# Merge gates in sixteen pieces inside two attentions, with levels, norms and old states reordered, in a decoder trunk

## The chip, the cores and the metric

The kernel runs on one core of a Trainium2 chip. TensorE (PE), VectorE (DVE), ScalarE (ACT), GpSimd (POOL) and SyncE (SP) each follow their own instruction list and meet at semaphores; SP's list here is a queue of DMA issues. The metric is the device time of one execution in microseconds. For the kernel before it is 1652.79 us, the median of 3 runs (1651.17 to 1656.56).

## The reference

One layer of a hybrid decoder for 256 prompt tokens and 8 x 4 sample tokens (288 rows of 1024, float32). The rows are multiplied by `W_in` (1024 x 5400), whose columns are the NSA queries, keys, values and branch gates, the HGRN2 parts `hq`, `hf`, `hi`, `hg`, and two merge gates of 1024 columns each. Then

```
a = NSA(z)     # compressed blocks + 16 selected blocks + window of 512, gated
b = HGRN2(z)   # gated linear recurrence, 4 heads of 128 x 128 states
h = LN1(alpha*x + (sig(g_a) * (a @ W_pa) + sig(g_b) * (b @ W_pb)) @ W_o)
y = LN2(alpha*h + MoE(h))   # router, top 4 of 32 experts, clamped SwiGLU
```

The sample tokens also read a paged cache (1024 past positions for each of 8 sequences) and an old HGRN2 state. The new states and cache rows are outputs too.

## The kernel before

The whole kernel is one hand-ordered list per engine; there is no planner. The order is what the code of each engine's block says, and waits on semaphores tie the lists together. The stages in TensorE's order:

- **Projection.** Eleven column blocks (`BLOCKS`) of 512 columns are loaded through three slots of `big`. A group (`GROUPS`) is one 128-column piece (turned: output columns on partitions, 288 tokens free; L633) or one token tile (L647; the 32 sample rows in four column groups, L641). Groups go through `NB` = 5 PSUM banks and are copied out by ACT or DVE. The last four blocks, `ga` and `gb`, are the merge gates: 16 groups, copied into `gates` by ACT (L1113).
- **HGRN2 levels.** The intra-chunk part is summed over seven levels (`LEVELS`). Level n needs, in turn: a difference on DVE (`half_diff`), Abs and Exp on ACT (L1146, L1148), one product on DVE (`hqF`, L1520) and one on GpSimd (`hkF`, L1344), the scores on TensorE (`level_scores`, L608), and mask and sum on DVE (`add_level`). `LEVEL_AFTER` puts the scores after every second merge gate group.
- **Compression.** Eight sequences in three sets (`CMP_SETS`). For each set pages are transposed (L675) and copied by both ACT (L1171) and DVE (L433), two hidden products for each of k and v (L688), Gelu on ACT, and small products for block keys and values.
- **HGRN2 states and outputs** (L728 to L768).
- **Prompt attention** in four steps `ITS` (query tile, head pair): `prompt_scores` (L810, and L813 for block scores), `prompt_max` on DVE, `prompt_exp` on ACT (eight row groups at L1207, four of 15 block columns at L1210), `prompt_weigh` on DVE, `prompt_turn` (L829, L832) with copies by ACT (L1219), `prompt_values`. In steps 2 and 3 `sample_gain` (L793) adds new keys to the old states, which GpSimd has decayed (L1358) and DVE adds up (`add_gain`, L1655); then the states are stored.
- **Sample attention** in two halves `s` of 16 tokens: small scores, twelve transposed key blocks (L886) and their scores, a selection on DVE after an importance product (L893), softmax over ACT and DVE, transposed probabilities (L904), values (L925), one last transpose (L928). SP loads the rows with `load_rows(0)` and `load_rows(1)` (L508: pages, L510: windows); the second waits for `pv_done` and for the stored old states.
- **Merge and output.** Eight column pieces (L940), gated by DVE (L1803), then `w_o` (L947) for three token tiles in two halves, residual (L1836), `norm` over all three tiles phase by phase (L1813 to L1828), transposes (L962), router product (L968), selection.
- **Experts.** 32 experts in a loop, each with four pairs of gate/up buffers (2 MB each) and four of down buffers (1 MB each). A buffer is loaded again when TensorE frees it (`gu_free`, `dn_free`, waited for by SP in `load_gu`, `load_dn`). Before the loop both semaphores are raised once `w_o` is through. L1027 is gate/up, L1057 down, `combine` (L1013) brings an expert's rows back and DVE adds them (`add_rows`, L1911).
- **Tail.** Three last combines, each waiting for the additions before it, `norm` on `y_rows`, three stores by GpSimd's queue.

## Time and profile before

| | |
|---|---|
| median of 3 runs | 1652.79 us (1651.17 to 1656.56) |
| profiled execution | 1650.89 us, span 1649.1 us |
| TensorE busy | 1455.6 us, 88% of the span |
| DVE, ACT, GpSimd busy | 431.8, 300.9, 80.5 us |
| moved from HBM | 471.54 MB |

The profile is one execution. Times are from the start of the span. A matmul of float32 is two records of TensorE, so that 32 records are 16 products. "Clock" is what the throttle granted of 2.4 GHz as a mean over the stretch (1.00 is 2.4 GHz, 0.50 would be 1.2 GHz). A row of busy time by stretch gives the stretch, its length, then the busy us (and instructions) of PE, PEld (weight load), DVE, ACT and POOL, the clock, the mean busy share of the DMA engines and GB/s. A row of groups by form gives line, engine and operation, out and in, and behind the bar its busy us and the mean ns of one, then idle time before it and what ended that. A releaser behind `<-` is the instruction whose semaphore ended a wait.

### The profile page before, as it was taken

The numbers are of one execution on the slowest core, as the hardware profiler recorded it, in microseconds if no ns is written. First come the engines' busy times: TensorE is split into PE (matmuls) and PEld (weight loads), VectorE is DVE, ScalarE is ACT, GpSimd is POOL, SyncE is SP. The second block draws the span as 40 slices with busy tenths as digits, with TensorE's granted clock in tenths as the row PEclk, the third lists the DMA queues.
The fourth block names the chain that finished last, engine by engine and source line by source line (L and its number), as shares of the span: only waits on it lengthen the run. The fifth ranks groups of instructions, "written<-read, shape, count | busy, mean of one in ns | idle before, by whom it ended". The sixth has DMA issues, their size and how long they took to land.

```text
span 1649.1 us, 20185 instructions
## 1 busy us (share of the span) xinstructions
PE 1455.6 (88%) x7423; PEld 654.3 (40%) x7423; DVE 431.8 (26%) x861; ACT 300.9 (18%) x545; POOL 80.5 (5%) x107
## 2 busy tenths in 40 slices
PE   6999988995755977999999999999999999999993
PEld 4757745574433624333333333323323323323321
DVE  0314432027422223221222212212212222222225
ACT  0103332014322012111111111111111111111111
POOL 0102300002000000000000000000000000000000
PEclk9999989997677996999999999999999999999997
DMA  6962120105155425999999999999999999999970
GB/s 235 335 212 103 32 77 23 29 22 175 33 165 151 160 92 233 420 417 417 418 416 418 419 414 418 418 417 418 417 415 418 412 405 419 409 405 419 410 313 30
DMA packets 116827, 476.52 MB, mean 289 GB/s; under 512 B 10451, under 2 KB 32275, under 8 KB 83827
## 3 DMA queue, kind: packets, MB, share of 16 engines
q1 hardware_dynamic: 112976, 465.78, 71.8%
q0 software_dynamic: 1856, 8.59, 1.5%
q10 hardware_dynamic: 1954, 1.63, 0.3%
q8 instruction: 24, 0.39, 0.1%
q14 instruction: 17, 0.13, 0.0%
HBM read 471.54 MB, written 8.59 MB: 291 GB/s over the span
## 4 chain that ended last, share of the span: by engine, by line
PE 49%; DMA 35%; DVE 8%; issue 2%; ACT 2%; SPq 2%; POOL 1%; DVEq 0%; ACTq 0%; POOLq 0%
DMA big<-in_w_gu 34%; PE bank L1027 14%; PE bank L688 7%; PE bank L633 5%; PE bank L1057 5%; PE bank L647 3%; PE bank L947 3%; PE bank L940 2%; PE bank L1013 2%; DVE big L433 1%; DVE work L1911 1%; PE bank L630 1%; DMA big<-in_w_in 1%; SPq L507 1%; SPq L508 1%
## 5 line engine op out<-in xcount | busy, mean ns | idle before, releaser
L1027 PE MATMUL bank<-big,gates 128*64 128x512 f32 x2048 | 451.1, 595 | 24.5 <-DMA big<-in_w_gu 23.7
L1027 PEld LDWEIGHTS bank<-big,gates 128*64 128x64 f32 x2048 | 142.1, 137 | 310.8 <-issue 257.1
L1057 PE MATMUL bank<-big,gates 128*64 128x512 f32 x1024 | 226.8, 595 | 0.0
L1911 DVE TENSOR_TENSOR work<-work,bank 128x512 f32<-128x512 f32 x198 | 127.0, 683 | 279.3 <-PE bank L1013 279.3
L1893 DVE TENSOR_SCALAR gates<-bank 128x512 f32<-128x512 f32 x32 | 22.1, 692 | 455.4 <-PE bank L1039 455.4
L1013 PE MATMUL bank<-gates 64*128 64x512 f32 x396 | 111.8, 641 | 21.0 <-DVE work L1911 21.0
L1057 PEld LDWEIGHTS bank<-big,gates 128*64 128x64 f32 x1024 | 70.7, 137 | 133.3 <-issue 133.3
L688 PE MATMUL bank<-big 128*128 128x417 f32 (+2 forms) x384 | 116.8, 464 | 4.6 <-DVE big L433 4.6
L1301 ACT ACTIVATE gates<-gates 128x512 f32<-128x512 f32 x32 | 20.2, 630 | 474.3 <-DVE gates L1893 474.3
L633 PE MATMUL bank<-xT,big 128*128 128x288 f32 x384 | 95.3, 407 | 0.0
L688 PEld LDWEIGHTS bank<-big 128*128 128x128 f32 x384 | 72.8, 191 | 46.5 <-issue 21.4
L1367 POOL TENSOR_TENSOR gates<-gates,nsaT 128x192 f32<-128x192 f32 x64 | 31.4, 511 | 1102.1 <-PE bank L1066 912.7
L633 PEld LDWEIGHTS bank<-xT,big 128*128 128x128 f32 x384 | 72.2, 190 | 20.0 <-issue 0.6
L994 PE MATMUL bank<-work,gates 128*64 128x512 f32 x264 | 65.5, 618 | 0.0
L1309 ACT ACTIVATE gates<-bank 128x512 f32<-128x512 f32 x32 | 19.1, 597 | 239.6 <-PE bank L1013 239.6
L1013 PEld LDWEIGHTS bank<-gates 64*128 64x128 f32 x396 | 29.8, 184 | 82.5 <-issue 51.9
L647 PE MATMUL bank<-big,xT 128*128 128x512 f32 (+1 forms) x128 | 51.5, 562 | 2.0 <-DMA big<-in_w_in 2.0
L947 PE MATMUL bank<-big,qT 128*128 128x512 f32 (+1 forms) x96 | 41.6, 593 | 1.5 <-DVE qT L1805 1.5
L1301 ACT ACT_TABLE_LOAD x32 | 41.1, 1283 | 0.6
L987 PE MATMUL bank<-work,gates 32*64 32x512 f32 x132 | 36.3, 627 | 3.0 <-DVE gates L1885 3.0
L647 PEld LDWEIGHTS bank<-big,xT 128*128 128x128 f32 x128 | 24.6, 194 | 26.5 <-issue 25.1
L1039 PE MATMUL bank<-kv,const 1*64 1x512 f32 x256 | 34.8, 613 | 0.0
(336 smaller groups left out, 1163.4 us busy)
## 6 DMA issues: line engine op xcount, KB each, us to landing
big<-in_w_gu SPq DMA_DIRECT2D x128, 2048.0 KB, 23.1
big<-in_w_dn SPq DMA_DIRECT2D x128, 1024.0 KB, 21.2
big<-in_w_in SPq DMA_DIRECT2D x10, 2048.0 KB, 14.7
big<-in_cache_cmp_kv SPq DMA_DIRECT2D x64, 128.0 KB, 2.5
big<-in_cache_slc_kv SPq DMA_DIRECT2D x64, 128.0 KB, 2.1
big<-in_cache_win_kv SPq DMA_DIRECT2D x8, 512.0 KB, 3.6
big<-in_w_o SPq DMA_DIRECT2D x1, 4096.0 KB, 12.9
out_win_s<-in_cache_win_kv POOLq DMA_DIRECT2D x1, 4064.0 KB, 6.9
```

The costliest lines, as they stand in the source:

```text
L633: last = pe.matmul(bank[:, 0:NT], w[:, k, n * P:(n + 1) * P], xTv[:, k, :], start=(k == 0), stop=(k == KD - 1))
L647: last = pe.matmul(bank[0:m, 0:cols], xTv[:, k, t0:t0 + m], w[:, k, 0:cols], start=(k == 0), stop=(k == KD - 1))
L688: last = pe.matmul(psum[3 + m][:, 0:n], w1[:, v, l, m * P:(m + 1) * P], XT[:, v, l % 8, l // 8:l // 8 + n], start=(l == 0), stop=(l == LP ...
L947: last = pe.matmul(psum[(4 + i) % 8][0:m, :], mixT[:, k, t0:t0 + m], w_o[:, k, (i % 2) * 512:(i % 2 + 1) * 512], start=(k == 0), stop=(k = ...
L987: pe.matmul(psum[0][half * CAP:(half + 1) * CAP, :], pick_rows[0:NS, 2, :], h_rows[0:NS, 2, half * 512:(half + 1) * 512], start=True, stop ...
L994: last = pe.matmul(psum[0][half * CAP:(half + 1) * CAP, :], pick_rows[:, t, :], h_rows[:, t, half * 512:(half + 1) * 512], start=False, st ...
L1013: last = pe.matmul(psum[6 + half][:, :], pgT[rows, t, :], ye[rows, :], start=True, stop=True)
L1027: last = pe.matmul(psum[2 + n][half * CAP:(half + 1) * CAP, :], xe[:, k % 4, (k // 4) * CAP:(k // 4 + 1) * CAP], gu_slot[k][:, c0:c0 + 512 ...
L1039: last = pe.matmul(psum[2 + n][half * CAP:(half + 1) * CAP, :], C("ones")[row, 0:CAP], bias[row, half * 512:(half + 1) * 512], start=False ...
L1057: last = pe.matmul(psum[5][half * CAP:(half + 1) * CAP, :], act_T[:, k % 4, (k // 4) * CAP:(k // 4 + 1) * CAP], dn_slot[k][:, half * 512:( ...
L1301: act.activation(sg, g_lim, ACT.Sigmoid, scale=1.702).then_inc(sg_ready, 1)
L1911: dve.tensor_tensor(y, y, psum[6 + half][:, :], ALU.add).then_inc(y_added, 1)
```

## The change

- The merge gates leave `BLOCKS`. They become 16 groups `gate_group(f)` of their own, f from 0 to 15, with weights in eight loads of 1 MB (`load_gates`, slots `wg_slot`). Gates 0 to 7 stand in the prompt attention and use bank 4 with DVE copying; gates 8 to 15 stand in the two halves of the sample attention, use bank 6, and ACT copies. Each waits for the copy of the one before (`fill_copied`). The sigmoid over all gates follows the last one.
- Level scores 0 to 2 stand between the `hi` and `hg` groups, 3 to 6 in the first compression set, between its pages and hidden products. Block keys and values use bank 7 and move one place later. The sets run over the sequences in another order (`CMP_ORDER`).
- The old states' `sample_gain` and `add_gain` stand ahead of `prompt_scores(0)`. Block scores of all four steps are made at once (`block_scores`, `block_shift`, one exponential, `block_weigh`) instead of within each step.
- SP loads selected rows per sequence (`load_rows(s, b4)`) and windows apart (`load_window`); the second half's rows overlay the old states and are split into those that wait for `state_p_stored` and those that wait for `states_stored`.
- `dn_free` is raised after the sample attention, half of `gu_free` after the merge, the other half after `w_o`.
- The sample rows of `w_o` run in four column groups at the start. The norms use `bn_stats` and `bn_aggr` tile by tile, in the order sample, prompt tile 0, prompt tile 1, beside `w_o`, transposes and router products. In the tail the last combines have banks of their own, norms run by tile, and SP stores.
- Several tiles move in SBUF to make room.

```diff
-CMP_SETS = [(0, 3), (3, 3), (6, 2)]
+CMP_SETS = [(5, 3), (2, 3), (0, 2)]
+CMP_ORDER = [b0 + n for b0, nb in CMP_SETS for n in range(nb)]
...
+LN_ORDER = [2, 0, 1]
+LAST_BANKS = [6, 2, 0]
...
           ("hf", C_HF, 512, True), ("hq", C_HQ, 512, True), ("hi", C_HI, 512, False),
-          ("hg", C_HG, 512, False), ("ga", C_GA, 512, True), ("ga", C_GA + 512, 512, True),
-          ("gb", C_GB, 512, True), ("gb", C_GB + 512, 512, True)]
+          ("hg", C_HG, 512, False)]
...
-LEVEL_AFTER = [n for n, g in enumerate(GROUPS) if g[0] in ("ga", "gb")][1::2][:len(LEVELS)]
+LEVEL_AFTER = [GROUPS.index(("hi", 5, 0)), GROUPS.index(("hg", 6, 0)), GROUPS.index(("hg", 6, 2))]
+NF = 2 * KD
...
+        wg_slot = [part(big, at, [KD, 2 * P]) for at in (8192, 10240, 8192, 10240, 20480, 22528, 8192, 10240)]
...
+            def load_gates(n):
+
+                sp.dma_start(wg_slot[n], ins["w_in"][0, :, C_GA + 2 * P * n:C_GA + 2 * P * (n + 1)].rearrange("(k p) n -> p k n", p=P))\
+                  .then_inc(w_loaded[1 + n % 2], 16)
+
+            sp.wait_ge(page_used, 6)
+            load_gates(0)
+            load_gates(1)
...
             sp.wait_ge(c_done, 6)
-            load_rows(0)
+            load_rows(0, 0)
+            load_rows(0, 1)
+            sp.wait_ge(fill_done, 2)
+            load_gates(2)
+            load_rows(0, 2)
+            sp.wait_ge(fill_done, 4)
+            load_gates(3)
+            load_rows(0, 3)
+            for b4 in range(4):
+                if b4 % 2 == 0:
+                    sp.wait_ge(fill_done, 6 + b4)
+                load_window(0, b4)
             sp.wait_ge(pv_done, len(ITS))
+            load_gates(4)
+            load_gates(5)
+            sp.wait_ge(state_p_stored, 16)
+            load_rows(1, 2)
+            load_rows(1, 3)
             sp.wait_ge(states_stored, 16 * DB)
-            load_rows(1)
-
+            load_rows(1, 0)
+            load_rows(1, 1)
+            sp.wait_ge(fill_done, 12)
+            for b4 in range(4):
+                load_window(1, b4)
+
+            sp.wait_ge(spv_done, 1)
+            load_gates(6)
+            load_gates(7)
...
             for k in range(KD // 2):
                 load_dn(0, 0, k)
-            for k in range(KD // 2):
+            sp.wait_ge(c_done, 6)
+            sp.dma_start(w_router[:, :, :], ins["w_router"][0].rearrange("(k p) n -> p k n", p=P)).then_inc(router_loaded, 16)
+            sp.dma_start(b_router, ins["b_router"].partition_broadcast(P).rearrange("p a n -> p (a n)")).then_inc(router_loaded, 16)
+            for k in range(KD // 4):
                 load_gu(0, 0, k)
...
+            sp.wait_ge(h_ready, 6)
...
+            for u in range(3):
+                turn_pages(u)
+                if u == 0:
+                    level_scores(3)
+                else:
+                    block_keys(2 * u - 1)
+                hidden(2 * u, 0)
+                if u == 0:
+                    level_scores(4)
+                hidden(2 * u, 1)
+                if u == 0:
+                    level_scores(5)
+                hidden(2 * u + 1, 0)
+                if u == 0:
+                    level_scores(6)
+                block_keys(2 * u)
+                hidden(2 * u + 1, 1)
 
...
-                    pe.wait_ge(ps_step, 5 * len(ITS))
-                    pe.wait_ge(ps_act, PREV_ACT[-1])
+                    pe.wait_ge(khat_ready, 3)
+                    pe.wait_ge(state_step, HH * (SEQ // CH))
...
+            def block_scores():
+
+                pe.wait_ge(state_step, HH * (SEQ // CH))
+                for it, (qt, hp) in enumerate(ITS):
+                    for hh in range(2):
+                        last = pe.matmul(psum[4][:, 4 * NCP * it:4 * NCP * (it + 1)].rearrange("p (g h c) -> p h g c", g=G, h=2)[:, hh, :, :],
+                                         qT[:, 0, 2 * hp + hh, qt * P:(qt + 1) * P], ckTp, start=True, stop=True)
+                last.then_inc(pcs_step, 1)
+
...
+            def gate_group(f):
+
+                pe.wait_ge(w_loaded[1 + f // 2 % 2], 16 * (f // 4 + 3))
+                pe.wait_ge(fill_copied, f + 1)
+                bank = psum[4 if f < 8 else 6]
+                for k in range(KD):
+                    last = pe.matmul(bank[:, 0:NT], wg_slot[f // 2][:, k, f % 2 * P:(f % 2 + 1) * P], xTv[:, k, :],
+                                     start=(k == 0), stop=(k == KD - 1))
+                last.then_inc(fill_done, 1)
...
+            block_scores()
+            sample_gain(0)
+            gate_group(0)
+            sample_gain(1)
             prompt_scores(0)
+            gate_group(1)
             prompt_scores(1)
             turn_outputs()
+            gate_group(2)
             for it in range(len(ITS)):
                 prompt_turn(it)
                 if it + 2 < len(ITS):
                     prompt_scores(it + 2)
-                else:
-                    sample_gain(it - 2)
                 prompt_values(it)
+                gate_group(3 + it)
+            gate_group(7)
...
+                pe.wait_ge(cc_step, 4 * s + 3)
+
+                pe.matmul(psum[0][:, 256:256 + NCS], C("same_group"), s_rows[:, 1600:1600 + NCS], start=True, stop=True).then_inc(cc_step, 1)
+                gate_group(8 + 4 * s)
+                gate_group(9 + 4 * s)
...
+                gate_group(10 + 4 * s)
+                gate_group(11 + 4 * s)
...
+            pe.wait_ge(spv_done, 4)
+            pe.sem_inc(dn_free, KD)
...
+            pe.wait_ge(ab_done, KD)
+            pe.sem_inc(gu_free, KD // 2)
...
-            for i in range(6):
-                t0, m = TILES[i // 2]
+            for k in range(KD):
+                for c in range(4):
+                    last = pe.matmul(psum[4][NS * c:NS * (c + 1), 0:D // 4], mixT[:, k, SEQ:NT], w_o[:, k, c * D // 4:(c + 1) * D // 4],
+                                     start=(k == 0), stop=(k == KD - 1), skip_group_check=True)
+            last.then_inc(wo_done, 1)
...
+            LOGIT_BANK = (1, 4, 5)
+            out_product(0)
+            out_product(1)
+            turn_h(0)
+            out_product(2)
+            pe.wait_ge(router_loaded, 32)
+            router_product(0)
+            out_product(3)
+            pe.wait_ge(wo_done, 5)
+            pe.sem_inc(gu_free, KD // 2)
+            turn_h(1)
+            router_product(1)
+            turn_h(2)
+            router_product(2)
...
+                for n, (b3, v, l) in enumerate(units[u]):
+                    turns = UNITS_BEFORE[u] + n
+                    act.wait_ge(xt_turned, turns + 1)
+                    copy_turned(lambda o, i: act.activation(o, i, ACT.Copy), u, b3, v, l, 0, turns).then_inc(xt_act, 1)
+
+            def gelu(q, m):
+
+                n = SET_N[q // 2]
+                if q:
+                    act.wait_ge(c_done, q)
+                act.wait_ge(hid_done, 2 * q + m + 1)
+                if q < 2:
+                    act.wait_ge(codes_copied, 2 * q + m + 2)
+                act.activation(hidT[:, m, 0:n], psum[3 + m][:, 0:n], ACT.Gelu_apprx_tanh,
+                               bias=pe_bias[:, q % 2, m:m + 1]).then_inc(gelu_done, 1)
...
+                copy_units(u)
+                if u == 0:
+                    level_decay(4)
+                    level_decay(5)
+                gelu(2 * u, 0)
+                if u == 0:
+                    level_decay(6)
+                gelu(2 * u, 1)
+                if u == 0:
+                    act.wait_ge(qf_ready, 6)
+                    act.wait_ge(kf_ready, 6)
+                    act.activation(hF[:, :, :], hb[:, :, :], ACT.Exp).then_inc(eb_ready, 1)
+                gelu(2 * u + 1, 0)
+                if u == 0:
+                    act.wait_ge(kd_diff, 2)
+                    act.activation(hkF[:, :, :], hkF[:, :, :], ACT.Exp).then_inc(kd_ready, 1)
+                gelu(2 * u + 1, 1)
...
+            act.wait_ge(pcs_step, 2)
+            act.activation(pcs, pcs, ACT.Exp, scale=SCALE).then_inc(pcs_step, 1)
             prompt_exp(0)
...
+                act.wait_ge(fill_done, f + 1)
+                act.activation(gatesT[:, f, :], psum[6][:, 0:NT], ACT.Copy).then_inc(fill_copied, 1)
...
                                    accum_out=stat[:, 3, 6 + n:7 + n]).then_inc(exp_done, 1)
+                    if n == 0:
+                        take_gates(8 + 4 * s)
...
+            def block_shift():
+
+                step = own.chain("pc_step", 0)
+                dve.wait_ge(pcs_step, 1)
+                mask = C("cmp_mask").rearrange("p (q c) -> p q c", q=2).unsqueeze(2).broadcast_to([P, 2, 8, NCP])
+                dve.tensor_tensor(pcs, psum[4][:, 0:16 * NCP].rearrange("p (q n c) -> p q n c", q=2, n=8), mask, ALU.add).then_inc(fill_copied, 1)
+                dve.wait_ge(fill_copied, 1)
+                step(dve.tensor_reduce(pc_stat[:, 0, :, :], pcs, AXX, ALU.max))
+                dve.tensor_tensor(pcs, pcs, pc_stat[:, 0, :, :].unsqueeze(3).broadcast_to([P, 2, 8, NCP]), ALU.subtract).then_inc(pcs_step, 1)
+
+            def block_weigh():
+
...
+            def take_gates(f):
+
+                dve.wait_ge(fill_done, f + 1)
+                dve.tensor_copy(gatesT[:, f, :], psum[4][:, 0:NT]).then_inc(fill_copied, 1)
+
+            block_shift()
+            add_gain(0)
+            take_gates(0)
+            add_gain(1)
             prompt_max(0)
+            take_gates(1)
             prompt_max(1)
+            block_weigh()
             outputs()
             for it in range(len(ITS)):
                 prompt_weigh(it)
+                take_gates(2 + it)
                 if it + 2 < len(ITS):
                     prompt_max(it + 2)
-                else:
-                    add_gain(it - 2)
                 prompt_out(it)
+            take_gates(6)
+            take_gates(7)
...
+            def norm_stats(rows, t, half):
+
+                m = TILES[t][1]
+                dve.bn_stats(ln_parts[0:m, t, half, :], rows[0:m, t, half * 512:(half + 1) * 512]).then_inc(own.next("ln_step"), 1)
+
+            def norm_scale(t, at):
+
+                m = TILES[t][1]
+                dve.wait_ge(own.semaphore, own.count)
+                dve.bn_aggr(ln_mean[0:m, t, :], ln_parts[0:m, t, :, :]).then_inc(own.next("ln_step"), 1)
+                dve.wait_ge(own.semaphore, own.count)
+                dve.tensor_scalar(ln_rstd[0:m, at % 3:at % 3 + 1], ln_mean[0:m, t, 1:2], LN_EPS, None, ALU.add).then_inc(ln_var, 1)
+
+            def norm_apply(rows, t, at, g, b, ready):
+
+                m = TILES[t][1]
+                rstd = ln_rstd[0:m, at % 3:at % 3 + 1]
+                dve.wait_ge(ln_rms, at + 1)
+                dve.reciprocal(rstd, rstd).then_inc(own.next("ln_step"), 1)
+                for half in range(2):
+                    cols = slice(half * 512, (half + 1) * 512)
+                    x = rows[0:m, t, cols]
+                    dve.scalar_tensor_tensor(out=x, in0=x, scalar=ln_mean[0:m, t, 0:1], in1=g[0:m, cols],
+                                             op0=ALU.subtract, op1=ALU.mult).then_inc(own.next("ln_step"), 1)
+                    dve.wait_ge(own.semaphore, own.count)
+                    dve.scalar_tensor_tensor(out=x, in0=x, scalar=rstd, in1=b[0:m, cols], op0=ALU.mult, op1=ALU.add).then_inc(ready, 1)
+
...
+            for at, t in enumerate(LN_ORDER):
+                for half in range(2):
+                    if at:
+                        i = 2 * (at - 1) + half
+                        x = h_rows[:, t, half * 512:(half + 1) * 512]
+                        dve.wait_ge(wo_done, i + 2)
+                        dve.scalar_tensor_tensor(out=x, in0=x, scalar=ALPHA, in1=psum[(5 + i) % 8][:, :], op0=ALU.mult, op1=ALU.add).then_inc(own.next("res_step"), 1)
+                        dve.wait_ge(own.semaphore, own.count)
+                    norm_stats(h_rows, t, half)
+                norm_scale(t, at)
+                norm_apply(h_rows, t, at, ln1[:, 0, :], ln1[:, 1, :], h_ready)
...
-            norm(y_rows, 1, ln2[0], ln2[1], y_ready)
+            for t in range(3):
+                dve.wait_ge(comb_done, rounds * (3 * NE) + t + 1)
+                if t == 0:
+                    dve.wait_ge(y_added, rounds * (6 * NE) + 6)
+                for half in range(2):
+                    y = y_rows[:, t, half * 512:(half + 1) * 512]
+                    dve.tensor_tensor(y, y, psum[LAST_BANKS[t] + half][:, :], ALU.add).then_inc(y_added, 1)
+                for half in range(2):
+                    dve.wait_ge(y_added, rounds * (6 * NE) + 7 + 2 * t + half)
+                    norm_stats(y_rows, t, half)
+                norm_scale(t, 3 + t)
+                if t:
+                    norm_apply(y_rows, t - 1, 2 + t, ln2[0], ln2[1], y_ready)
+            norm_apply(y_rows, 2, 5, ln2[0], ln2[1], y_ready)
```

## Rows read from the trace of the kernel before

**Rows 1.** The page: span, and the chain that ended last by engine.
```profile
span 1649.1 us, 20185 instructions
...
PE 49%; DMA 35%; DVE 8%; issue 2%; ACT 2%; SPq 2%; POOL 1%; DVEq 0%; ACTq 0%; POOLq 0%
```

**Rows 2.** Busy time of the engines by stretch, eight of the stages.
```profile
125.70:203.50 77.80, 76.35 (x396) 61.59 (x392) 37.65 (x49) 23.88 (x33) 24.88 (x9) 1.00 0.21 68
203.50:368.00 164.50, 145.51 (x622) 95.47 (x622) 31.53 (x59) 36.35 (x52) 0.00 (x0) 0.96 0.12 35
...
381.60:451.30 69.70, 41.64 (x238) 27.32 (x235) 39.05 (x116) 33.64 (x124) 9.51 (x7) 0.66 0.28 84
451.30:486.60 35.30, 22.04 (x210) 15.51 (x210) 9.25 (x33) 11.91 (x24) 4.13 (x6) 0.76 0.58 167
486.60:533.00 46.40, 21.35 (x211) 14.40 (x211) 8.43 (x29) 12.01 (x24) 0.00 (x0) 0.71 0.52 143
...
607.30:634.20 26.90, 12.93 (x72) 11.90 (x72) 15.69 (x27) 9.34 (x17) 0.00 (x0) 0.59 0.97 389
634.20:652.20 18.00, 10.15 (x34) 5.40 (x34) 6.76 (x28) 4.88 (x9) 0.97 (x2) 0.57 0.29 120
1619.00:1649.10 30.10, 3.39 (x12) 0.90 (x12) 18.08 (x27) 5.12 (x10) 1.65 (x3) 0.62 0.11 39
```

**Rows 3.** The chain of waits in the expert loop: start, length, piece.
```profile
652.22 13.95 PE bank L1027 x64
...
1541.83 26.69 DMA big<-in_w_gu
...
1572.50 26.52 DMA big<-in_w_gu
```

**Rows 4.** Timeline of TensorE and ScalarE, and groups by form (busy us, mean ns).
```profile
59.97 15.79 PE L633 MATMUL bank<-xT,big 128*128 128x288 f32 x64
...
L1344 POOL TENSOR_TENSOR work<-work 128x1152 f32<-128x1152 f32 x6 | 22.8, 3795 | 105.1 <-ACT work L1148 99.8 <-PE bank L608 5.3
...
204.78 4.04 ACT L1154 ACTIVATE gates<-gates 128x4608 f32<-128x4608 f32 x1
208.84 1.28 ACT L1158 ACT_TABLE_LOAD   x1
210.14 1.16 ACT L1158 ACTIVATE work<-work 128x1152 f32<-128x1152 f32 x1
...
249.63 22.70 PE L688 MATMUL bank<-big 128*128 128x417 f32 x64
```

**Rows 5.** Groups by form: decay, addition of gains, block scores.
```profile
L1358 POOL TENSOR_TENSOR big<-big,work 128x1024 f32<-128x1024 f32 x4 | 7.6, 1932 | 1.2 <-PE bank L768 1.2
...
L1655 DVE TENSOR_TENSOR big<-big,bank 128x512 f32<-128x512 f32 x8 | 5.0, 683 | 12.2 <-PE bank L793 12.2
...
L813 PE MATMUL bank<-xT,qT 128*128 128x30 f32 x16 | 3.4, 342 | 0.0
```

**Rows 6.** Waits of TensorE, 381 to 533 us: in total, times, longest.
```profile
PE bank L904 <- DVE work L1783: 17.8, 2, 8.9
PE bank L832 <- DVE small L1704: 17.0, 4, 5.7
PE bank L886 <- DMA big<-in_cache_win_kv: 12.9, 1, 12.9
```

**Rows 7.** Timeline of SP's queue: issue of eight selected pages.
```profile
488.65 8.03 SPq L508 DMA_DIRECT2D big<-in_cache_slc_kv  x8
```

**Rows 8.** Sample rows: w_o product by form, projection on the timeline.
```profile
L947 PE MATMUL bank<-big,qT 128*32 128x512 f32 x32 | 13.9, 593 | 0.0
...
108.01 1.95 PE L641 MATMUL bank<-big,xT 128*32 128x128 f32 x64
```

**Rows 9.** Router product in the chain, and a reduction by form.
```profile
626.14 7.97 PE bank L968 x48
...
L1813 DVE TENSOR_REDUCE small<-work 128x1 f32<-128x1024 f32 x4 | 4.8, 1212 | 0.0
```

585 lines of the change are left out of this document (287 added, 298 removed).

## The prediction

> **What bounds the kernel now.** I read the page first: TensorE is busy 88% of the span, and the chain that ended last is half TensorE and a third weight transfers [rows 1]. That average mixes two parts, so the next view is the busy time by stage [rows 2]. Up to 652.2 us the kernel is one chain through projections, compression, two attentions, merge, norm and router; after it come 32 experts. The chain of waits shows what sets the second part: from the middle of the loop on, experts follow each other 30.7 us apart, each waiting 26.5 us for its last gate/up transfer [rows 3]. The expert loop is therefore a transfer stream in the end. But the stream can only run on once expert 0 frees its first buffers, 3.8 us after it starts, and all eight buffer pairs are full by then in both versions. So the loop is a block of fixed length hung on expert 0's first matmul at 652.2, and a microsecond gained ahead of that is one gained in the end.
>
> In the front part the stages differ [rows 2]: 125.7 to 203.5 TensorE is full (76.4 of 77.8 us, clock 1.00, that is 2.4 GHz), with 16 merge gate groups and seven level scores. In the prompt attention (381.6 to 451.3) it works 41.6 of 69.7 us, in the sample attention (451.3 to 533.0) 43.4 of 81.7, at a mean clock of 0.66 to 0.76, which is partly the 1.2 GHz level. That is about 66 us of idle TensorE for 62 us of gates.
>
> **Part by part.** *Gates leave the projection.* Four groups take 15.8 us [rows 4], so one 3.9 and sixteen 62.4. The levels (77.8 - 62.4 = 15.4 us, 1.4 of it waiting) stay; three go between hi and hg groups, four between the first hidden products. Is there time for their chain there? One level costs a GpSimd product of 3.8 us, a difference of 1.4 (as long as the DVE product beside it), then Abs and Exp of 1.16 each with a table load of 1.28 [rows 4]: 8.8 us against 13.2 us for a hidden product (half of the 22.7 us of a pair) and a score. It fits, and the merge sigmoid (4.0 us and its table load) no longer stands ahead of the page copies. Reordering block keys into the shadow of page copies fills more. TensorE idled 19.0 us in 203.5 to 368.0, 20.4 with the 1.4 above. Following copies, levels and products through in the new order leaves me 12.0, so the stage gives 62.4 + 8.4 = **70.8 us**. Bounds: all of the 20.4 gone (74.8 with the 8 us that I do not expect), or each level late.
>
> The new order switches between Gelu and Exp, six table loads more. Rows have 1.28 us for each, with the activation starting 1.3 us after the one before [rows 4], and they lie beside products. The Trainium skill (ScalarE: Activation LUTs, What ACT_TABLE_LOAD costs) counts 2.66 us for each switch, drain included; no row here shows the 1.38 us of drain. By that figure the last switch alone would delay the next page copies by about 1.4 us, and the sum would be 72.0.
>
> *Old states in front of the prompt attention.* GpSimd's decay takes 7.6 us [rows 5] after the HGRN outputs. It was hidden; now sample_gain(1) waits for add_gain(0), which waits for it, and prompt_scores(0) waits for both: 7.8 and 0.8 to the end of add_gain(0), 1.4 for sample_gain(1) (as it takes where it stands now), 2.5 for add_gain(1) [rows 5]: 12.5 us, with block scores and gate 0 inside. Behind that stands a chain on DVE and TensorE. Gate 1 delays prompt_scores(1), and gate 2 the first transposes, by 3.9 each. Gates 3 to 5 lie in waits for the weighing of 3 to 6 us [rows 6]; 1.7 stay uncovered. Gates 6 and 7 have nothing beside them, since DVE copies gate 7 before it makes q_own: 8.6. Back come the two add_gains out of steps 2 and 3 (5.0), the block columns' exponentials (eight ACT instructions fewer per step, of which I let 1.0 count, four times) and their scores on TensorE, 3.4 [rows 5]. 12.5 + 3.9 + 3.9 + 1.7 + 8.6 - 5.0 - 4.0 - 3.4 = 18.2, so 69.7 becomes 87.9: **-18.2**. Bounds: if gates 1, 2, 6 and 7 run at 1.2 GHz, 15.6 more; above, rival (a).
>
> *Sample attention.* After the importance product TensorE waited 8.9 us, twice, for the probabilities [rows 6]. Two gates of 7.8 would fit, but both use bank 6, and ACT copies the first only between its two exponentials: the second starts 21.1 us into the half and ends at 25.1, where the transposes began at 23.0, so 2.1 late. Gates 10, 11 (and 14, 15) stand after the values, ahead of the last transpose, uncovered: 8.3 each half. One wait disappears: 12.9 us for the second half's rows [rows 6]. They were issued after the old states were stored, each eight pages taking 8.0 us of SP's queue and over 1 for what is between [rows 7]. Now the states are stored long before; but SP comes to these rows only past gate 7, for which the first half's last windows wait. Its 32 pages then take 37 us, and their first use is 47 us later. The windows, which wait for gate 11, have the 5 us of eight key transposes. The first half goes from 35.3 to 45.7, the second from 46.4 to 43.9, both together from 81.7 to 89.6: **-7.9**. Of the other new items in SP's queue, eight gate loads of 1 MB, the tightest two follow those windows: landed some 11 us into the second half, due at 14. Merges: the sigmoid (5.3 us) runs beside the first one and delays the first mix by 0.4, nothing behind it: 0.
>
> *w_o.* The 32 sample rows took 32 records, 13.9 us of 41.6 [rows 8]. In four column groups of 32 they are like the projection's 64 records over 128 columns in 1.95 us [rows 8]; at 256 columns 3.6. Added inside: transposes and router product of the sample tile, 2.1. 41.6 becomes 33.5: **+8.1**.
>
> *Norm and router.* 26.9 us at 607.3 [rows 2]. Now only tile 1 is left after the last product: residual 0.7, statistics 0.7, small steps and root 1.0, halves 1.4 and 1.4, so 5.2. TensorE's own chain is as long by then and goes on: tile 0's transposes 2.6, its copy and router product 3.5 (three took 8.0 [rows 9]), tile 1's transposes and copy 2.0, product 2.7: 10.8. **+16.1**. bn_stats is in no row: for 512 columns I take 0.7, half of a 1.2 us reduction over 1024 [rows 9] and a start; bounds 0.2 and 1.3.
>
> *Tail.* Three combines waited for each other's additions, then came whole-tile norms: 30.1 us from 1619.0 [rows 2]. Now additions 3 x 1.3, statistics 3 x 1.4, small steps 3 x 0.5, two passes over 3 x 1024 columns 3 x 3.0, and the first combine: 19 to 20 us, then 5.3 to store as before. 30.1 to 25.6: **+4.5** (bounds +8.5 and +1 by bn_stats).
>
> Sum: 70.8 - 18.2 - 7.9 + 8.1 + 16.1 + 4.5 = 73.4. The profiled execution took 1650.9 us (1.8 beyond its span), giving 1577.5; it lies 1.9 below the median of the runs, 1652.8, giving **1579**.
>
> **Rivals.** (a) *The clock gives more back.* TensorE is at 85% in the prompt stage then, and stretches like that show 0.90 to 1.00 [rows 2]. A third of some 25 us would come off the path: 8 us, 1571. The Trainium skill (TensorE: Matmul & The Clock Gate, HAM oscillation) says that idle waits between bursts bring the lower clock back; the trace agrees, with 0.66 in the stage with the most short waits. Against: most waits of the path are DVE's and ACT's. 0.13.
> (b) *SP's queue is late.* If the pages take the pace of a full queue, the 12.9 us wait returns before the second half: 1592. For: a slack of 10 us after a schedule of four steps. 0.07.
> (c) *The levels starve TensorE.* A GpSimd product and a table load late for each of three levels, 3 x 5.1 = 15: 1594. For: ACT and DVE do page copies and levels in one order, so that each waits for the other. 0.07.
> (d) *No gain past the loop*: if the transfer stream and not expert 0's start sets the end, only the tail's 4.5 is left, 1648. Against: the stream stands still from 635 to 656 (DMA share 0.29 in 634.2 to 652.2 [rows 2]). 0.02.
> (e) *Slower.* The gates run at 1.2 GHz (7.8 us each) and wholly uncovered, 124 us, in attentions that also pay 12.5 for the states, and SP's wait stays. Against 95.0 of gains ahead and behind and 4.5 in the tail: 124.8 + 12.5 - 99.5 = 38, 1691. It decides from an average of 5.4 us uncovered per gate; I count 2.4. 0.01.
>
> **How the numbers follow.** The forecast keeps 0.70, 1579, own range 1567 to 1591. To take in (b) and (c) the range goes to 1599, and to 1564 for (a) and bn_stats together. A measurement of this kernel tells 0.3%, 5 us, from no change: faster 0.97, same 0.02 (case d), slower 0.01 (case e).
>
> **What would show it.** HGRN outputs done near 311 us; prompt stage of 85 to 90 us; no wait of TensorE on the second half's rows; merges from about 488; end of the last w_o product near 554; expert 0's first matmul near 583; from there to the last combine 967 us as before. A wait over 3 us of a hidden product on DVE, or a loop longer than before, would make it wrong.

## The result, and the profile of the changed kernel

The changed kernel takes 1569.4 us (median of 4 runs, 1560.36 to 1572.06) beside 1654.67 us of the kernel before: 0.9477 of it, 95% interval 0.9432 to 0.9521. In a second set on one chip it was 1562.78 us (5 runs) beside 1649.91 (9 runs), 0.9477 again, interval 0.9459 to 0.9496. The profiled execution took 1560.36 us, 9.0 below the first median; it is the one that is taken apart here, against the 1650.89 us of the profile before, a difference of 90.5. Between the medians the difference is 85.3 us, and 87.1 in the second set.

The page, span and chain by engine, against [rows 1]:

```profile
span 1558.6 us, 20255 instructions
...
PE 51%; DMA 37%; DVE 6%; ACT 3%; issue 2%; POOL 1%; SPq 0%; DVEq 0%; ACTq 0%
```

Busy time by stretch. The columns are those of [rows 2], and the stretches are the prompt attention, the two halves of the sample attention, `w_o`, norm and router, selection, and the tail from the last expert's first combine:

```profile
305.93:390.64 84.71, 65.42 (x361) 45.53 (x361) 43.18 (x118) 29.26 (x93) 13.80 (x12) 0.92 0.36 106
390.64:433.60 42.96, 34.73 (x275) 24.28 (x275) 9.26 (x33) 12.97 (x28) 0.00 (x0) 0.96 0.56 172
433.60:476.34 42.74, 36.09 (x275) 25.39 (x275) 8.43 (x29) 13.48 (x29) 0.00 (x0) 0.92 0.70 195
509.12:542.06 32.94, 32.94 (x152) 15.44 (x152) 13.17 (x23) 3.71 (x9) 0.00 (x0) 1.00 0.39 156
542.06:552.58 10.52, 8.06 (x49) 7.07 (x48) 5.59 (x14) 3.65 (x6) 0.00 (x0) 0.76 0.88 342
552.58:570.58 18.00, 10.04 (x34) 5.40 (x35) 6.76 (x28) 4.89 (x9) 0.97 (x2) 0.57 0.09 35
1537.55:1558.60 21.05, 2.84 (x12) 1.07 (x12) 16.97 (x33) 1.75 (x5) 0.00 (x0) 0.66 0.15 56
```

TensorE is now busy 136 of 170 us in the two attentions, where it was 85 of 151, and the granted clock of the prompt attention and the two halves went from 0.66, 0.76 and 0.71 to 0.92, 0.96 and 0.92. The selection is as long as before, 18.0 us. The chain of waits: first products of expert 0, and last wait for gate/up weights, against [rows 3]:

```profile
570.58 13.95 PE bank L1177 x64
...
1490.69 26.84 DMA big<-in_w_gu
```

Expert 0 starts 81.6 us earlier (570.58 against 652.22), and from there to the last expert's first combine it takes 967.0 us, before 966.8. What was gained ahead of the loop arrives in full, as a shift of the whole loop.

### The profile page after: what moved, and what is told of

It is laid out like the page before. It is cut to its first block, busy times and chain, and to the rows that moved or that the text cites. A ratio compares the mean times of both kernels' runs of the same rounds, so it can differ in the third digit from the quotient of the medians.

```text
span 1558.6 us, 20255 instructions
## 1 busy us (share of the span) xinstructions
PE 1428.3 (92%) x7455; PEld 641.0 (41%) x7455; DVE 434.6 (28%) x875; ACT 299.1 (19%) x508; POOL 77.9 (5%) x104
## 4 chain that ended last, share of the span: by engine, by line
PE 51%; DMA 37%; DVE 6%; ACT 3%; issue 2%; POOL 1%; SPq 0%; DVEq 0%; ACTq 0%
DMA big<-in_w_gu 36%; PE bank L1177 15%; PE bank L755 7%; PE bank L1207 5%; PE bank L704 3%; PE bank L920 3%; PE bank L1065 2%; PE bank L688 2%; PE bank L1080 2%; PE bank L1163 2%; PE bank L685 1%; DVE work L2139 1%; DMA big<-in_w_in 1%; PE bank L1136 1%; PE bank L663 1%
## 5 line engine op out<-in xcount | busy, mean ns | idle before, releaser
L2139 DVE TENSOR_TENSOR work<-work,bank 128x512 f32<-128x512 f32 x192 | 123.1, 683 | 275.5 <-PE bank L1163 275.5
L755 PEld LDWEIGHTS bank<-big 128*128 128x128 f32 x384 | 72.1, 189 | 39.6 <-issue 19.7
L920 PE MATMUL bank<-xT,big 128*128 128x288 f32 x256 | 71.3, 436 | 8.1 <-ACT gates L1377 7.2
L920 PEld LDWEIGHTS bank<-xT,big 128*128 128x128 f32 x256 | 50.8, 204 | 26.9 <-issue 13.2
L1143 PEld LDWEIGHTS bank<-work,gates 128*64 128x64 f32 x264 | 16.3, 138 | 45.3 <-issue 45.3
```

What stands on the lines that cost most here:

```text
L755: last = pe.matmul(psum[3 + m][:, 0:n], w1[:, v, l, m * P:(m + 1) * P], XT[:, v, l % 8, l // 8:l // 8 + n], start=(l == 0), stop=(l == LP ...
L920: last = pe.matmul(bank[:, 0:NT], wg_slot[f // 2][:, k, f % 2 * P:(f % 2 + 1) * P], xTv[:, k, :], start=(k == 0), stop=(k == KD - 1))
L1143: last = pe.matmul(psum[0][half * CAP:(half + 1) * CAP, :], pick_rows[:, t, :], h_rows[:, t, half * 512:(half + 1) * 512], start=False, st ...
L2139: dve.tensor_tensor(y, y, psum[6 + half][:, :], ALU.add).then_inc(y_added, 1)
```

## The experiments

The stage lengths of each run are differences of times of its own trace: end of the HGRN outputs, first small scores of each half, first merge product, expert 0's first product. The first label letter separates single edits (e) from combinations and the repeated run (f).

Experiments 1 to 7 and the first combination are one execution each, so stage lengths are compared and not whole times. How far a stretch varies that no edit touches can be read from the same traces: the prompt attention took 84.6 to 86.1 us in four executions of the same instructions, the first half 42.9 to 43.0 and the second 41.2 to 43.3. Smaller differences than these are not read as effects.

**1. How much of the gates is covered, and what the clock does.** In `gate_group` seven of the eight products of each gate are left out:

```diff
-                for k in range(KD):
-                    last = pe.matmul(bank[:, 0:NT], wg_slot[f // 2][:, k, f % 2 * P:(f % 2 + 1) * P], xTv[:, k, :],
-                                     start=(k == 0), stop=(k == KD - 1))
-                last.then_inc(fill_done, 1)
+                pe.matmul(bank[:, 0:NT], wg_slot[f // 2][:, 0, f % 2 * P:(f % 2 + 1) * P], xTv[:, 0, :],
+                          start=True, stop=True).then_inc(fill_done, 1)
```

> Each of the sixteen gate groups makes one of its eight products (seven eighths of the gates' matmuls are left out; loads, copies, order and waits stay). By my steps 38.9 us of the gates are uncovered (18.1 in the prompt attention, 20.8 in the sample attention), so seven eighths of that, 34 us, should go: prompt attention 84.7 to 69, sample attention 85.7 to 67. By the clock theory the gates are what keeps TensorE at 2.4 GHz: without them the granted clock of the two attentions falls from 0.92 to 0.96 to some 0.7, the other products run longer again (256-column scores 389 to some 640 ns, transposes of probabilities 277 to some 430 ns), and only 20 to 25 us go. By the theory that the gates are all uncovered, 54 us go.

The whole took 1547.46 us, and the attentions 80.8, 37.9 and 39.0, so 157.7 instead of 170.4 us: only 12.7 gone, less than every case had expected (34, 20 to 25, or 54). Busy time by stretch of this kernel, and four groups by form (the gates first; busy us, mean ns):

```profile
304.72:385.48 80.76, 48.73 (x250) 30.26 (x249) 42.65 (x118) 29.71 (x93) 13.80 (x12) 0.72 0.36 111
385.48:423.40 37.92, 26.35 (x218) 17.91 (x218) 9.25 (x33) 13.42 (x28) 0.00 (x0) 0.74 0.59 185
423.40:462.44 39.04, 26.45 (x218) 17.61 (x219) 8.42 (x29) 13.60 (x29) 0.00 (x0) 0.74 0.81 223
```

```profile
L919 PE MATMUL bank<-xT,big 128*128 128x288 f32 x32 | 13.9, 522 | 14.9 <-ACT gates L1375 14.0 <-DVE gates L1916 0.6 <-DVE small L1891 0.3
...
L901 PE MATMUL bank<-kT,qT 64*128 64x256 f32 x32 | 7.1, 615 | 0.0
...
L1023 PE MATMUL bank<-const,work 128*128 128x128 f32 x24 | 5.8, 430 | 1.9 <-DVE work L1995 1.9
...
L1044 PE MATMUL bank<-big,work 128*32 128x128 f32 x192 | 10.0, 402 | 0.0
```

The same groups in the changed kernel, with the gates and the statistics instruction between them:

```profile
L901 PE MATMUL bank<-kT,qT 64*128 64x256 f32 x32 | 4.0, 389 | 0.0
...
L920 PE MATMUL bank<-xT,big 128*128 128x288 f32 x256 | 71.3, 436 | 8.1 <-ACT gates L1377 7.2 <-DVE gates L1918 0.6 <-DVE small L1893 0.3
...
L1025 PE MATMUL bank<-const,work 128*128 128x128 f32 x24 | 3.4, 277 | 0.5 <-ACT work L1407 0.5
...
L1046 PE MATMUL bank<-big,work 128*32 128x128 f32 x192 | 5.7, 274 | 0.0
...
L2024 DVE BATCH_NORM_STATS2 small<-work 128x6 f32<-128x512 f32 x8 | 5.3, 687 | 0.1
```

The 256-column scores take 615 against 389 ns, transposes of the probabilities 430 against 277, values 402 against 274. TensorE's busy time without the gates is 136.2 - 71.3 = 64.9 us in the changed kernel, 101.5 - 13.9 = 87.6 with one product of eight, and 85.0 before the change. So the gates bring 57 us of products and take 23 us off the others by keeping TensorE mostly at its upper level (2.4 GHz) through the attentions. The 23 us are of the size of what is missing, 34 less 12.7. A second size, with four of the eight products left out, to see how the clock follows:

```diff
-                for k in range(KD):
+                for k in range(KD // 2):
```

> Each gate group makes four of its eight products (half of the gates' matmuls left out). Leaving out seven eighths made the two attentions only 12.8 us shorter (80.8, 37.9 and 39.0 us), with granted clocks of 0.72 to 0.74. If my cover were right and the clock no matter, half of the gates would take 38.9 / 2 = 19 us away. By the clock theory the products that are left are too few to keep the clock: it falls to some 0.8, the other products get longer in part, and the attentions are 5 to 9 us shorter than with whole gates; a transpose group of the probabilities takes more than 277 ns in at least one half.

1551.37 us; the attentions took 80.7, 37.5 and 39.8, so 158.0:

```profile
305.87:386.61 80.74, 56.17 (x298) 36.73 (x297) 42.76 (x118) 29.49 (x93) 13.82 (x12) 0.81 0.37 112
386.61:424.11 37.50, 27.32 (x243) 18.38 (x243) 9.26 (x33) 12.98 (x28) 0.00 (x0) 0.91 0.61 187
424.11:463.89 39.78, 29.06 (x243) 19.81 (x243) 8.43 (x29) 13.47 (x29) 0.00 (x0) 0.87 0.79 219
```

Taking away the first half of the products saves 12.4 us, taking away three quarters of the other half nothing more (157.7), while the granted clock goes on from 0.81, 0.91 and 0.87 to 0.72, 0.74 and 0.74. By covers alone it would be 19 and 34. The 5 to 9 us of my expectation were too little: at half size the clock is still mostly up, and the other products take 112.6 - 40.9 = 71.7 us, from there to the eighth 16 us more.

For the prompt attention the chain that ended last tells how this splits. With whole gates it holds 22.2 us of gates, 21.5 of other products and 30.8 of DVE and ACT. With one product of eight it holds 1.4, 33.2 and 34.5, and 1.7 of SP's queue. So 20.7 us of gates left the chain, and 11.7 came back as other products, 3.7 as DVE and ACT, 1.7 as SP. Of the 11.7, 7.4 are the same groups on both chains running longer (prompt scores 6.6 to 11.2 us, gains 1.2 to 2.1, values 5.1 to 7.0). For the sample attention the split stays open. There TensorE waited 7.2 us for ScalarE's gate copies with whole gates, 11.1 and 14.0 with short ones, and the second half waits for its pages, as shown below.

The gates' row by form at half size:

```profile
L920 PE MATMUL bank<-xT,big 128*128 128x288 f32 x128 | 40.9, 470 | 12.0 <-ACT gates L1377 11.1 <-DVE gates L1918 0.6 <-DVE small L1893 0.3
```

In both kernels something else shows for the first time, a wait of TensorE for the second half's pages. At half size it is 2.1 us:

```profile
PE bank L1005 <- DMA big<-in_cache_slc_kv: 2.1, 1, 2.1
```

With one product of eight it is 1.5. The first half is then 37.5 and 37.9 us long, and SP's queue, which turns to the 32 pages once gate 7 is through, needs longer than that with the last landing. So the queue and no longer the products bounds the start of the second half. A part of the missing time is this wait.

**2. The old states' update, moved back alone.**

```diff
-            sample_gain(0)
             gate_group(0)
-            sample_gain(1)
             prompt_scores(0)
...
                     prompt_scores(it + 2)
+                else:
+                    sample_gain(it - 2)
```

(and `add_gain` on DVE in the same way, with the waits that belong to it).

> Only the old states' update goes back to steps 2 and 3 of the prompt attention; gates, levels and loads stay. By my steps it cost 12.5 us in front and gave back 5.0, so the prompt attention gets 7.5 us shorter, 84.7 to 77; the states are then stored near 381 us, and SP's queue comes to the rows that overlay them only some 17 us after the end of gate 7, near 400, so nothing of the 12.9 us wait comes back and the whole is 7.5 us shorter. Rival: the move was what removed the wait, and without it the second half waits again for its rows, 5 to 13 us, so that the whole is no shorter or longer.

The prompt attention took 80.4 us, 4.3 less than 84.7 and not 7.5; the halves 42.8 and 43.0; no wait for rows. Expert 0 starts 3.5 us earlier; the run took 1559.94 us, only 0.4 below the changed kernel's profile, because its loop was 3.0 us longer (970.0; how much the loop varies stands under experiment 8). TensorE's timeline at the start of the stage, first here and then in the changed kernel:

```profile
309.00 5.81 PE L921 MATMUL bank<-xT,big 128*128 128x288 f32 x16 [1.33 <-DVE small L1895]
314.74 1.16 PE L902 MATMUL bank<-kT,qT 64*128 64x128 f32 x16
```

```profile
305.86 1.97 PE L910 MATMUL bank<-small,qT 128*128 128x30 f32 x16
307.75 1.14 PE L884 MATMUL bank<-gates,big 32*128 32x512 f32 x8
309.15 4.12 PE L920 MATMUL bank<-xT,big 128*128 128x288 f32 x16 [0.25 <-DVE small L1893]
314.62 1.14 PE L884 MATMUL bank<-gates,big 32*128 32x512 f32 x8 [1.35 <-DVE big L1840]
318.36 1.61 PE L901 MATMUL bank<-kT,qT 64*128 64x128 f32 x16 [2.60 <-DVE big L1840]
```

In the changed kernel 12.5 us pass from the start of the block scores (305.86) to the first prompt scores (318.36), as the prediction summed them. Without the states 9.0 remain (305.70 to 314.74), because gate 0 and the block scores had been inside and now stand alone. Back in steps 2 and 3 the update costs 0.8 us (steps of 12.1 and 11.5 instead of 11.6 and 11.2) and not 5.0: there it lies in waits. 3.5 less 0.8 is 2.7 of the 4.3 us. The other 1.6 are the products right behind the states: in the changed kernel the first prompt scores took 1.61 us and gate 1 5.33, here the same two took 1.16 and 4.15, at the durations of the upper level. So the move is a small loss by itself, and it is not what removed the 12.9 us wait: SP came to these rows only after gate 7 in either order.

**3. Levels 3 to 6 ahead of the pages.** `level_scores(3)` to `(6)`, their decays and DVE's `level_step` stand in a row before the first page.

> Level scores 3 to 6 stand in a row before the pages' transposes, with their decays and products; everything else stays. If levels beside compression are what the stage's gain rests on, each of four levels shows its chain of 8.8 us (GpSimd product, difference, Abs, Exp) before its scores, less the 5.4 us that the page copies wait for the level work now: 25 to 30 us more before the HGRN states. If they are in the way of the page copies as much as they are hidden, 10 us or less.

1588.33 us, and the HGRN outputs end 27.7 us later (333.68 against 305.93). Waits of TensorE in 125 to 190 us (in total, times, longest):

```profile
PE bank L663 <- DVE nsaT L1652: 13.3, 2, 6.7
PE bank L663 <- DVE nsaT L1655: 8.4, 1, 8.4
PE bank L663 <- POOL work L1501: 4.0, 1, 4.0
```

The level chain shows 10.5, 10.4 and 7.8 us from one score to the next, and the scores themselves run at the lower level (1.2 GHz; the granted clock of 130 to 174 us is 0.65), 3.75 us instead of 1.95. The place beside the hidden products is worth the 25 to 30 us that were expected.

**4. The stores of y.** The three issues go back from SP to GpSimd's list.

> The three stores of y go by GpSimd's queue as before the change; the rest of the tail stays. If the tail's gain beyond my 4.5 us is the store queue, the stretch from the last VectorE instruction to the end grows from 2.4 to 5.3 us and the tail from 21.0 to 23.9. If it is VectorE's work, the end stays at 2.4 us after the last instruction.

1565.54 us, and 23.95 us from the first last combine to the end instead of 21.05. Last DVE instruction and last store of this kernel:

```profile
1557.67 0.74 DVE L2045 SCALAR_TENSOR_TENSOR work<-work,small,hg 32x512 f32<-32x512 f32 x1
```

```profile
1558.70 0.51 POOL L1537 DMA_DIRECT2D out_y_s<-work  x1 [2.37 <-DVE work L2045]
```

and of the changed kernel:

```profile
1555.47 0.74 DVE L2046 SCALAR_TENSOR_TENSOR work<-work,small,hg 32x512 f32<-32x512 f32 x1
```

```profile
1556.23 0.33 SPq L631 DMA_DIRECT2D out_y_s<-work  x1
```

From the start of the last DVE instruction to the end of the span it is 6.0 us here and 3.1 there. The queue that issues the store is worth 2.9 us. The Trainium skill (DMA: Bandwidth & Descriptors, Latency and other measured facts) gives a first byte after about 1 us by GpSimd's path and 0.6 by the other; the 2.9 us here are more than that difference.

**5. A second bank for gates 9 and 13.**

```diff
-                pe.wait_ge(fill_copied, f + 1)
-                bank = psum[4 if f < 8 else 6]
+                if f not in (9, 13):
+                    pe.wait_ge(fill_copied, f + 1)
+                elif f == 13:
+                    pe.wait_ge(snsa_copied, 2)
+                bank = psum[GATE_BANK[f]]    # 7 for 9 and 13
```

> Gates 9 and 13 write a bank of their own (7, free until the values), so they no longer wait for ScalarE to copy gates 8 and 12. In the changed kernel each waits 3.0 us, and the transposes of the probabilities start 3.4 us after the probabilities are ready. If that wait is what makes the gates late, each half becomes 3.4 us shorter, 6.8 in all (43.0 and 42.7 to 39.6 and 39.3). If VectorE's softmax sets the start anyway, nothing changes.

The waits of the changed kernel in 306 to 571 us that this and the next edit aim at:

```profile
PE bank L920 <- ACT gates L1377: 7.2, 4, 3.0
PE bank L869 <- DVE work L1827: 6.0, 1, 6.0
PE bank L901 <- DVE big L1840: 2.6, 1, 2.6
```

1553.68 us. The first half took 39.6 us as expected, the second 41.9. Two rows of TensorE's timeline, the first transposes of the probabilities and the second half's first key transposes:

```profile
409.79 1.09 PE L1029 MATMUL bank<-const,work 128*128 128x128 f32 x8 [1.39 <-DVE work L2001]
...
429.34 4.74 PE L1009 MATMUL bank<-const,big 128*128 128x128 f32 x20 [1.25 <-DMA big<-in_cache_slc_kv]
```

The probabilities' transposes now wait 1.39 us for DVE, where before DVE's result waited for TensorE. The second half lost most of its gain to the pages' transfer: TensorE waits 1.25 us, and the 20 transposes behind it take 4.74 us, 4.24 in the changed kernel. Its 41.9 us lie within the 41.2 to 43.3 that it takes unchanged, so only the first half's gain is shown here; experiment 8 shows 39.6 us with the transfers nearly in time. Of the whole time's 6.7 us below the changed kernel's profile, 3.0 lie ahead of the attentions, where nothing was changed.

**6. Scores ahead of the gates in the prompt attention** (on top of the kernel of experiment 2).

```diff
             block_scores()
-            gate_group(0)
             prompt_scores(0)
-            gate_group(1)
+            gate_group(0)
             prompt_scores(1)
+            gate_group(1)
```

(DVE: `prompt_max(0)`, gate 0, `prompt_max(1)`, `block_weigh`, gate 1.)

> On the kernel with the states' update back in steps 2 and 3: scores of step 0 ahead of gate 0, scores of step 1 ahead of gate 1, and VectorE copies gate 1 after the maximum of step 1. VectorE then no longer waits for gates 0 and 1 before its maxima, and the first transposes of probabilities should start some 5 us earlier: prompt attention 80.4 to 75. If TensorE and not VectorE is the limit there, 1 us or less.

1552.16 us; the prompt attention took 74.5 us, 5.9 less than without it. The transposes of the HGRN outputs, and the first of the probabilities (333.84 without the edit):

```profile
320.32 0.66 PE L869 MATMUL bank<-const,work 128*128 128x128 f32 x4 [2.21 <-DVE work L1829]
...
327.54 1.04 PE L941 MATMUL bank<-const,work 128*128 128x128 f32 x8
```

**7. Levels one place later.**

```diff
                 turn_pages(u)
-                if u == 0:
-                    level_scores(3)
-                else:
-                    block_keys(2 * u - 1)
+                if u == 1:
+                    level_scores(6)
+                if u:
+                    block_keys(2 * u - 1)
                 hidden(2 * u, 0)
                 if u == 0:
-                    level_scores(4)
+                    level_scores(3)
```

(4 and 5 in the same way, ACT's decays and DVE's steps with them.)

> Only level scores 3 to 6 and their decays move one place later (3, 4, 5 behind the first three hidden products, 6 behind the second set's pages), so that VectorE copies all pages of the first set before it turns to level 3. The 5.4 us for which the page transposes wait for VectorE should go, and the HGRN outputs end 5 us earlier. Rival: the level chain then comes late behind the hidden products, and the wait turns up there.

The row of the changed kernel, and the same place here:

```profile
144.23 2.79 PE L737 MATMUL bank<-const,big 128*128 128x128 f32 x12 [5.40 <-DVE big L446]
```

```profile
136.75 2.60 PE L737 MATMUL bank<-const,big 128*128 128x128 f32 x16 [0.30 <-PE bank L737]
140.91 11.45 PE L755 MATMUL bank<-big 128*128 128x417 f32 x32 [1.55 <-DVE big L446]
```

From the first page to the end of the HGRN outputs it is 166.8 us instead of 173.7: 6.9 gone. Of the 5.4 us wait 1.55 are left, ahead of the first hidden product, and none stands behind the hidden products. The first page stood 1.4 us earlier too, and yet only 4.4 of the 8.3 reach expert 0 (1559.58 us): the attentions take 3.0 us more and what lies behind the merge 0.9, although nothing in them was changed. Their products are the same and some run longer (gate 1 took 6.19 us here, 5.33 in the changed kernel). The granted clocks are 0.90, 0.92 and 0.92 here and 0.92, 0.96 and 0.92 there, so the clock falls at other moments. The prompt attention's part of it, 1.7 us, also comes without any edit: the kernel of experiment 4 took 86.1 us there at 0.90.

**8. Together.**

> The states' update back, the prompt order, the second bank and the later levels in one kernel. Each alone took away 3.5, 5.9, 3.4 to 4.2 and 6.9 us ahead of the experts; if they are independent, merges start 21 us before those of the changed kernel (476.3) or somewhat more, near 452, and the profiled time is near 1537. By the queue theory they are not: SP issues the second half's 32 pages only after gate 7, for 39 us, so that with a first half of 39.6 us TensorE waits for them again, 2 to 4 us, and its clock falls behind that wait; merges start near 455.

1538.6 us; stages of 74.1, 39.6 and 39.6 us, merges from 450.65. The gains add up: merges start 25.7 us earlier, 1.7 of it already ahead of the first page. The pages were not late, against the queue theory as I had it. SP's row:

```profile
373.10 36.95 SPq L529 DMA_DIRECT2D big<-in_cache_slc_kv  x32
```

It ends at 410.05, and the second half's first key transposes start at 411.88: 1.8 us after the last issue, which is just what the last page needs (median 2.0 us from issue to landing). For the pages the queue is at its limit there, not over it. The four windows, issued behind them, do come late, by a little:

```profile
419.26 0.63 PE L1011 MATMUL bank<-const,big 128*128 128x128 f32 x4 [0.85 <-DMA big<-in_cache_win_kv]
```

> As the combined kernel, and GpSimd's queue issues half of the second half's pages (those over the old states, once these are stored), and VectorE makes the sample queries' operand of each half ahead of the last gate copy and ahead of the value copy. By the queue theory the wait for the pages is gone; with 1.4 and 1.6 us from the operand the merges start near 449, 27 us before the changed kernel's, and the median is some 27 us below its: 1542. If GpSimd issues its pages at a slower pace than SP (1.2 us each), a wait for rows shows in the second half.

1542.31 us (5 runs, 1535.45 to 1545.1), 0.9346 of the kernel before (0.9328 to 0.9365). Merges from 451.52: not earlier than without it. First half 37.9, second 42.2, with one wait in it:

```profile
418.94 0.63 PE L1010 MATMUL bank<-const,big 128*128 128x128 f32 x4 [2.39 <-DMA big<-in_cache_win_kv]
```

So the pages had been moved out of the way in vain: with them in front the windows had been issued from 410.10 us on, without them from 409.30, since they wait for gate 11. The operand that VectorE makes earlier shortens the prompt attention, 72.0 us instead of 74.1, but expert 0 starts no earlier (545.76 against 545.79 us).

```diff
-            sp.wait_ge(fill_done, 12)
             for b4 in range(4):
-                load_window(1, b4)
+                sp.wait_ge(fill_done, 10 + 2 * (b4 // 2))
+                load_window(1, b4, rows_loaded[0] if b4 >= 2 else win_loaded)
```

> As the combined kernel with GpSimd's pages, and the second half's first two windows wait only for gate 9, whose weights they overlay, the other two for gate 11 as before. In the kernel without this TensorE waited 2.4 us for the windows and its second half took 42.2 us against 37.9 of the first. If the windows behind gate 11 are the cause, the wait goes, the second half takes 39.5 us or less, merges start near 449 and the median is 2 to 3 us below 1542. If the last two windows bind, the wait is only smaller. If the transfers of the loop hide it, the median stays within 2 us.

1534.0 us (6 runs, 1530.38 to 1536.49), 0.9285 of the kernel before (0.926 to 0.931); second half 38.8 us, merges from 446.32. The median is 8.3 us below 1542 where 2 to 3 were expected. The second half gives 3.4 us of it; 1.9 us lie ahead of the attentions, where nothing was changed, and the rest is not found in the profiles. The longest waits of TensorE in 295 to 460 us are now none of a transfer:

```profile
PE bank L1032 <- DVE work L2013: 2.8, 2, 1.4
PE bank L867 <- DVE work L1841: 2.5, 2, 2.2
PE bank L942 <- DVE work L1892: 1.7, 1, 1.7
```

This version beats both kernels: its interval (0.926 to 0.931) lies below the changed kernel's of the second set (0.9459 to 0.9496).

> The changed kernel itself, unchanged, beside the two: 1560 to 1572 as in its runs so far, and the length of the expert loop from the first matmul to the last combine (967.0 in its profile, 966.8 before, up to 970.0 in the experiments) shows what the transfers alone vary by.

1562.78 us (1561.68 to 1568.77), loop 968.5 us. Its profiled execution has all stages ahead of 550 us within 0.7 us of the first one's, and is 2.4 us longer; the row that shows why, against 570.58 and 13.95 above:

```profile
571.48 15.28 PE bank L1177 x64
```

By the end of expert 0's gate/up products 2.2 of the 2.4 us are there, 0.9 ahead of them and 1.3 in them: the same products ran longer, at a granted clock of 0.91 instead of 1.00. In the profiles of this study the loop took 967.0 to 970.6 us.

## Why the prediction held, step by step

The forecast was 1579 us in a range of 1564 to 1599, faster; it is 1569.4. The mechanisms held in the main, and the sizes that were off were off to the same side: in the profiled execution the terms give 90.5 us instead of 73.4, and nothing cancelled. That the median still lies 9.6 and not 17 us from the forecast is in part luck, since the profiled execution was the fastest of its four; the second set's median, 1562.78, lies 1.2 us below the range. By terms, in the profiled execution (forecast, then measured):

| term | forecast | measured |
|---|---|---|
| projection and compression | +70.8 | +75.7 |
| prompt attention | -18.2 | -15.1 |
| sample attention | -7.9 | -4.0 |
| merge products | 0 | 0 |
| `w_o` | +8.1 | +8.6 |
| norm and router | +16.1 | +16.4 |
| selection and loop | 0 | -0.1 |
| tail | +4.5 | +9.05 |
| sum | 73.4 | 90.5 |

**Bound and shift: right.** The loop is a block hung on expert 0's start; rival (d) is out, 81.5 us of 81.6 arrived at the last expert's combine (1619.04 against 1537.55).

**Projection and compression: right in mechanism, 4.9 short.** Levels stand beside hidden products without a wait, which experiment 3 prices at 27.7 us; rival (c) is out. TensorE's waits from the first page copies to the HGRN outputs sum to some 10.6 us against my 12.0, most of it one wait of 5.4 us that I did not see: DVE turns to level 3 amid the page copies (experiment 7). The hidden products over 417 columns took 514 ns instead of 529: 45.6 us busy in 128 records instead of 47.1. The rest is not taken apart. The upper bound of 74.8 was too low and was passed: with all of the 20.4 us gone the stage would give 62.4 + 20.4 = 82.8.

**Prompt attention: the sum was nearly right, two of its terms were not.** 12.5 us for the states is what the trace shows, and by the clock they cost 1.6 more behind them (experiment 2). "Back come the two add_gains (5.0)" was wrong: it is 0.8, since they lay in waits (experiment 2). And the step that let gates count at 3.9 us with everything beside them at the durations of before was wrong in kind: experiment 1 shows that gates change what the other products cost. Without seven eighths of them 34 us should have gone and 12.7 went, and the others took 23 us more. Rival (a) had the mechanism, with 8 us; the two attentions came 7.0 us under the forecast. That these 7.0 are the clock's is argued from sizes: the other products took 85.0 us there before and 64.9 after, and how much of the 20 us lay on the chain was not measured. Rival (a) was given 0.13, and it deserved more: the 0.66 to 0.76 of [rows 2] beside 1.00 where TensorE is full was the evidence. The Trainium skill (TensorE: Matmul & The Clock Gate, HAM oscillation) says that idle waits between bursts bring the lower clock back; the clock of 0.72 to 0.74 without most of the gates agrees.

**Sample attention: right in place, 3.9 too dear.** Each first gate pair ran 3.4 us past the probabilities (2.1 forecast), by the wait for ACT's copy that the prediction named; experiment 5 takes it away. With that the halves should have taken 47.0 and 45.2 us; they took 43.0 and 42.7. What was too dear is again the other products, taken at the durations of before: without the gates TensorE was busy 16.6 and 17.9 us in the halves, before 22.0 and 21.4. The rows were in time, as said, but with 3.6 us from SP's last issue to the first use instead of 10, and the last page's landing takes 2.1 of them: rival (b) did not come true, and three of the four versions whose first half is shorter by 3.4 us or more without a change to the loads show it in small (1.25, 1.5, 2.1 us); the fourth, the first combination, waits 0.85 us for the windows behind the pages.

**`w_o`, norm, router: right** within 0.5 us each. `bn_stats` over 512 columns takes 0.69 us, forecast 0.7.

**Tail: the place right, the size half.** DVE's part took 18.7 us (1537.55 to 1556.2) as against the 19 to 20 that were summed; what was mis-sized is "then 5.3 to store as before": the store went to SP's queue, and from there it takes 2.4 after DVE's last instruction. I had counted the moved store at nothing. The other 1.6 us of the difference lie in DVE's part, of which 20.3 had been carried into the sum.

**The marks.** Of the marks in the prediction, the HGRN outputs (311, measured 305.9), merges (488, 476.3), the end of `w_o` (554, 542.1) and expert 0 (583, 570.6) all came early by the terms above; the prompt stage (85 to 90) missed by 0.3; no wait on the second half's rows and a loop of 967 us came as said. No hidden product waited for DVE; the 5.4 us wait of the compression was a page transpose's.

**Table switches.** The prediction weighed 1.28 us for each against 2.66 of the Trainium skill (ScalarE: Activation LUTs, What ACT_TABLE_LOAD costs). In the changed kernel's trace ScalarE's Exp of level 1 starts at 104.14, 1.3 us after the Abs before it ended; no time for a drain shows beside the load.

## What to carry to other kernels

Work that fills short waits of TensorE has a price and a gift: price it together with what the other products cost at the granted clock of a full stretch, not at that of the stretch as it was. When a stage gets shorter, compare the time of its transfers' last issue with their first use, queue by queue; here 3.6 us of slack lay behind 39 us of issues, and the windows behind them were late as soon as it was used up. A moved DMA is moved in two ways, in time and in queue, and the queue alone was worth 2.9 us at the end of the kernel.
